# The third dense piece of the odd pairs in a forgetting attention layer moves from behind the fourth tile's transposes to before them

## What is computed

```python
def odd_mixer(h, w_in, b_f, qnorm_g, knorm_g, w_out):
    proj = (h @ w_in).astype(jnp.float32)
    q, k, v, g, fl = jnp.split(proj, [FOX_WIDTH, 2 * FOX_WIDTH, 3 * FOX_WIDTH, 4 * FOX_WIDTH], axis=-1)
    q = rms_norm(hd(q), qnorm_g).transpose(0, 2, 1, 3)
    k = rms_norm(hd(k), knorm_g).transpose(0, 2, 1, 3)
    logf = jax.nn.log_sigmoid(fl + b_f.astype(jnp.float32))
    cumf = jnp.cumsum(logf, axis=1).transpose(0, 2, 1)
    for blk in range(s_ // FOX_BLOCK):
        ...
        logits = (jnp.einsum('bhqd,bhkd->bhqk', q[:, :, q0:q1], k[:, :, :q1]) * scale
                  + cumf[:, :, q0:q1, None] - cumf[:, :, None, :q1])
        mask = jnp.arange(q0, q1)[:, None] >= jnp.arange(q1)[None, :]
        probs = jax.nn.softmax(jnp.where(mask, logits, -jnp.inf), axis=-1)
        outs.append(jnp.einsum('bhqk,bhkd->bhqd', probs, v[:, :, :q1]))
    o = jnp.concatenate(outs, axis=2).transpose(0, 2, 1, 3).reshape(b_, s_, FOX_WIDTH)
    o = o * jax.nn.silu(g)
    return o.astype(h.dtype) @ w_out
```

## Time and profile before

| what | value |
|---|---|
| median of 3 runs | 1705.82 us (1705.78 to 1706.29) |
| the profiled execution's own time | 1707.55 us |
| its span, first to last instruction | 1705.8 us |
| mean granted TensorE clock | 0.998 |
| TensorE matmuls busy | 1687.0 us, 99% |
| TensorE weight loads busy | 1396.9 us, 82% |
| VectorE, ScalarE, GpSimd busy | 1040.8, 759.3, 807.7 us |

### The profile page before, as it was taken

How to read it: one execution, slowest core, us unless ns; L and a number is a source line. 1 busy time by engine, 2 the same in 40 slices (tenths; PEclk the granted TensorE clock), 3 DMA queues, 4 the chain that set the end, 5 groups by cost and what they waited for, 6 DMA issues and landing times.

```text
span 1705.8 us, 25667 instructions
## 1 busy us (share of the span) xinstructions
PE 1687.0 (99%) x9753; PEld 1396.9 (82%) x9753; DVE 1040.8 (61%) x1717; ACT 759.3 (45%) x1332; POOL 807.7 (47%) x617
## 2 busy tenths in 40 slices
PE   9999999999999999999999999999999999999999
PEld 7777788888888888888888888887877888887887
DVE  5887567555564872664475555678377844237752
ACT  4443644222222354664532222234544457666650
POOL 6635236555555473232465555553532335453342
PEclk9999999999999999999999999999999999999999
DMA  9735237444445243222274444442322133334522
GB/s 369 253 138 201 84 124 271 173 170 164 163 158 194 99 136 112 87 83 92 98 272 173 172 172 172 172 165 82 99 75 69 51 100 100 106 89 129 160 89 74
DMA packets 114833, 242.72 MB, mean 142 GB/s; under 512 B 6144, under 2 KB 27776, under 8 KB 114736
## 3 DMA queue, kind: packets, MB, share of 16 engines
q1 hardware_dynamic: 112560, 237.20, 40.3%
q10 hardware_dynamic: 2176, 4.19, 0.8%
HBM read 239.21 MB, written 2.16 MB: 141 GB/s over the span
## 4 chain that ended last, share of the span: by engine, by line
PE 87%; DVE 6%; DMA 2%; ACT 2%; issue 1%; POOL 1%; SPq 0%; DVEq 0%; POOLq 0%; ACTq 0%
PE bank L242 40%; PE bank L656 20%; PE bank L1674 5%; PE bank L1640 3%; PE bank L453 3%; PE bank L432 2%; PE bank L1642 2%; DMA ct<-cumd 1%; PE bank L1758 1%; PE bank L416 1%; PE bank L1722 1%; PE bank L1234 1%; PE bank L1746 1%; PE bank L2253 1%; DVE fP L1850 1%
## 5 line engine op out<-in xcount | busy, mean ns | idle before, releaser
L2755 POOL TENSOR_TENSOR wsp<-raw,wsp 128x512 fp32r<-128x512 f32 x516 | 761.7, 1508 | 803.4 <-ACT wsp L197 803.4
L242 PE MATMUL bank<-xT,wsp 128*128 128x512 f32 x2016 | 464.9, 390 | 0.0
L242 PEld LDWEIGHTS bank<-xT,wsp 128*128 128x128 f32 x2016 | 377.7, 188 | 80.0 <-issue 0.9
L197 ACT ACTIVATE wsp<-raw 128x1024 fp32r<-128x1024 f32 x131 | 138.8, 1060 | 464.0 <-PE bank L656 240.3
L656 PE MATMUL bank<-wsp,hT 128*128 128x512 f32 x1344 | 308.2, 389 | 0.0
L242 PE MATMUL bank<-wsp,xT 128*128 128x512 f32 x1248 | 299.9, 396 | 1.3 <-DVE tok L2519 0.9
L656 PEld LDWEIGHTS bank<-wsp,hT 128*128 128x128 f32 x1344 | 252.3, 188 | 52.4
L242 PEld LDWEIGHTS bank<-wsp,xT 128*128 128x128 f32 x1248 | 231.8, 189 | 54.8 <-issue 4.8
L874 DVE CUSTOM_DVE_ANT_0 ada_ring<-ada_ring,crow,cols 128x1024 f32<-128x1024 f32 x96 | 148.4, 1580 | 4.5 <-DMA ada_ring<-in_ada_rows 4.5
L200 ACT ACTIVATE wsp<-raw 128x1024 fp32r<-128x1024 f32 x131 | 137.2, 1047 | 0.0
L795 DVE TENSOR_TENSOR x<-bank,x 128x512 f32<-128x512 f32 x80 | 55.2, 690 | 110.5 <-PE bank L656 110.5
(11 more groups left out here) (351 smaller groups left out, 2161.1 us busy)
## 6 DMA issues: line engine op xcount, KB each, us to landing
raw<-in_ff_w SPq DMA_DIRECT2D x64, 1024.0 KB, 5.2
ada_ring<-in_ada_rows SPq DMA_DIRECT2D x96, 512.0 KB, 6.3
tok<-in_ada_rows SPq DMA_DIRECT2D x32, 512.0 KB, 5.5
raw<-in_odd_w_in SPq DMA_DIRECT2D x16, 1024.0 KB, 5.4
raw<-in_gla_w_in SPq DMA_DIRECT2D x12, 1024.0 KB, 7.2
raw<-in_att_w_in SPq DMA_DIRECT2D x12, 1024.0 KB, 5.2
raw<-in_even_w_in SPq DMA_DIRECT2D x12, 1024.0 KB, 5.2
ring_s<-in_ada_rows SPq DMA_DIRECT2D x16, 512.0 KB, 11.0
```

The source lines that it names most:

```text
L197: act.activation(home[:, 0, 0:HK // 2], raw[:, slot, 0:HK // 2], ACT.Copy).then_inc(hi_part, 1)
L242: mm = pe.matmul(out_ap, l, r, start=(start and a == b), stop=(stop and a == 1))
L2755: ins = pool.tensor_tensor(w[:, 1, k], raw[:, slot, k], w[:, 0, k].bitcast(F32), ALU.subtract)
```

## The change

In the forgetting layer the third dense piece of a pair always stands between the third and the fourth tile's transposes. Before, it stood there only where the piece was a quarter of a tile (`quarters`, pairs 0, 2, 4 and 6), and behind all transposes otherwise.

```diff
                 quarters = u + 2 in work and work[u + 2][6] - work[u + 2][5] == KT // ST
                 for w in range(u, u + ST):
-                    if w == u + 3 and quarters:
+                    if w == u + 3 and (quarters or not ahead):
                         dense(u + 2)
                     turned(w)
-                if not quarters:
+                if not quarters and ahead:
                     dense(u + 2)
                 dense(u + 3)
```

## The result

| | before | after |
|---|---|---|
| median of 20 runs | 1705.93 us | 1708.64 us |
| lowest to highest | 1704.02 to 1709.86 | 1706.59 to 1710.48 |
| profiled execution, its own time | 1707.55 us | 1709.76 us |
| its span | 1705.8 us | 1708.0 us |

The ratio of the two kernels is 1.0014, with a 95% interval of 1.0008 to 1.0021: the change costs 2.4 us, between 1.4 and 3.6. The forecast was 1.8 us and "within 0.2%"; 1.8 us lies inside that interval, so the times alone don't tell it from 2.4. The medians themselves lie 2.7 us apart. The runs of one kernel spread over 4 to 6 us, far more than the 0.5 us of the three runs that I had seen.

A forecast was written before the change was run, and what follows sets the result against it. TensorE, busy for 99% of the span, was taken as the bound. Pairs 1, 3, 5 and 7 add 0.72 + 0.37 + 0 + 0.72 = 1.81 us to the median of 1705.82, giving 1707.6 us; range 1706.1 to 1709.0.

The forecast's parts named there:

- the delay of pair 5 is not absorbed: Rival, 15%: pair 5's delay reaches the end, +0.75 us and up to 0.8 of transfer either way, 1708.4 us.
- an unchanged 1.1 us wait in pair 7 with the end later by 2.5: Sign of a wrong forecast: pair 7's wait for VectorE stays 1.1 us and the end comes 2.5 us later.
- The wait for VectorE is not hidden: Third tile's transposes wait for all four tiles (shared PSUM banks), so the moved piece covers no wait; gain 0.
- The cut: One more transpose block and dense block in each changed pair, costing 0.14 + 0.23 = 0.37 us.
- A free cut: Rival, 10%: matmul spacing depends on columns alone, only uncovered transposes in pairs 1 and 7 cost; 0.7 us, 1706.5.
- weight loads and row groups: TensorE: the skill page lets a weight load run beside a matmul only where row groups differ; no size given.
- The wait for the bank: Moved piece waits for bank 0: about 0.34 us in pair 1, none in pair 3; pair 7 delayed about 0.72 us.
- Pair 5 costs nothing: Pair 5's delay of about 0.75 us shortens pair 7's 1.1 us VectorE wait to about 0.4; net cost 0.
- The clock: Granted clock was 1.00 in pair 2, which is cut the same way, so nothing was added; no chance of its own.
- The late copy: Rival, 4%: ScalarE's late copy of tiles 3 and 4 stalls scores in pairs 2, 4, 6; 4.5 us, 1710.3.

The follow-up runs named there:

- filled: Against the kernel with only pair 7 moved: eight extra 128 x 128 TensorE matmuls between pair 7's first and second tiles' transposes; ratio 1.0008 (0.9999 to 1.0017).
- the bias loads first: Pair 7's bias loads issued before the output weights' transfer: kernel before 0.9997, no piece between 1.0001, changed kernel 1.0007.

## Why the prediction was right, and where not

The direction, the class and most of the places were right; the size was 0.6 us short, though the interval holds the forecast too. The measured median of 1708.64 us lies inside the range of 1706.1 to 1709.0, but 1.0 us above the forecast and nearer to the 1708.4 of the rival *the delay of pair 5 is not absorbed*. The prediction also named its own sign of being wrong, an unchanged 1.1 us wait in pair 7 with the end later by 2.5, and the first profile shows very nearly that: 1.15 us, and an own time that is 2.2 us longer. So two terms that were put at 0, pair 5 and the clock, failed, and the range held because it left room for the first; for the second it left none, and that is luck.

- *The wait for VectorE is not hidden*: right. It stands before the third tile's transposes in all five profiles with pair 7 moved and not filled, at 0.83 to 1.15 us, and before 4 transposes instead of 16.
- *The cut*: right. 0.31 us in pair 3 (forecast 0.37), and 0.36 to 0.38 when taken away in pairs 2, 4 and 6. A free cut is refuted here. The prediction took that rule from the Trainium skill, TensorE: Matmul & The Clock Gate (Back-to-back issue gap); the page gives the spacing by columns alone for an isolated matmul and says that in a stream the weight load counts too, so what failed is the use made of it. What the prediction says of weight loads and row groups stands in that page's section The mechanism; no term of the sum rests on it.
- *The wait for the bank*: right. A wait of 0.26 us in pairs 1 and 7, and the piece starts 0.60 us after the third tile does. From the third tile on, pair 1 costs 0.67 us (6.98 against 6.31) and pair 7 0.70 (9.34 against 8.64), with 0.72 forecast for each (the terms given for pair 7 add up to 0.70). The whole of pair 1 took 15.39 to 15.93 us moved and 14.60 to 15.00 not moved; the 0.2 us beyond the cut is a longer wait for VectorE ahead of the moved piece, where the kernels are the same. In both, the 12 transposes that ran under the gate before now stand behind it.
- *Pair 5 costs nothing*: partly wrong. Moving it costs 0.73 us locally (18.10 to 18.33 against 17.41 to 17.53), as forecast. But what pair 7 gives back varied: from its scores to the third tile it took 8.61 to 9.74 us in the five profiles with pair 5 moved, 9.27 in the mean, and 9.37 to 9.82, 9.61 in the mean, in the seven others. That is 0.3 us returned of 0.73, so pair 5 costs about 0.4 us instead of 0. The two ranges overlap and the profiles are few, so 0.4 is an estimate and anything from nearly nothing to the whole 0.73 us fits. The step that failed took the wait of 1.1 us in one execution for steady slack. It isn't: bias loads that land later, or VectorE's low part beside GpSimd, take it up. Nor was all of the wait slack: 8.61 us from pair 7's scores to its third tile is what is left when the mask holds nothing (pair 5 alone), and that leaves a wait of 0.37 us, so the slack before was 9.44 - 8.61 = 0.83 us, just enough for pair 5's 0.73. The mask is part of the trouble as well: it took 1.93 to 1.99 us in the nine profiles in which VectorE's L2145 ran beside it, and 1.48 or 1.49 in the four in which it was done or nearly done by then. The chain of waits in the changed kernel shows the later landing:

```profile
1598.68 0.36 SPq L2158
...
1600.11 8.44 DMA ct<-cumd
...
1615.04 6.81 DMA ct<-cumd
...
1623.47 5.43 POOL wsp L2755 x4
1628.92 0.37 SPq L166
1629.34 1.35 SPq L2158
...
1631.83 7.92 DMA ct<-cumd
```

  Against the earlier trace rows, the first transfer is 0.44 us longer, the second 0.35 shorter and the last 0.45 longer. The conversion is 0.42 longer, but the mask before it took 1.48 us instead of 2.02, so that goes even. One issue took 1.35 us where it took 0.51, all four together 2.96 instead of 2.34. From pair 5's issue to pair 7's mask it is 41.5 us instead of 40.4. With pair 7's mask that late, nothing is absorbed. Whether the moved piece itself makes the chain longer stays open: it is 40.31 to 41.52 us in the four profiles with pair 5 moved and the old order of the loads, and 40.09 to 40.68 in the six others.
- *The clock*: wrong. I took the clock of pair 2, cut in the same way, and added nothing. But pair 2 waits for only 0.28 us. That can't be all, though. Pair 0 of the kernel before has nearly the two waits of the moved pair 7 (its second is the 0.26 us of the earlier trace rows), and keeps its clock; here its third tile, and the 3.68 us from its piece to the next scores:

```profile
1546.10 0.34 PE L1746 MATMUL bank<-ident,fP 64*128 64x64 f32 x4 [1.01 <-DVE fP L1859]
```

```profile
1546.70:1550.38 3.68, 3.68 (x26) 2.54 (x26) 2.00 (x4) 1.04 (x2) 0.17 (x1) 1.00 0.88 239
```

  The same stands in all eleven profiles with that piece between, 1.01 or 1.02 and 0.26 us, and the clock read 1.00 in each. What tells the two pairs apart, the 0.1 us of the first wait or the 12 dense matmuls before it instead of 24, was not tested. In pair 7 the granted clock fell in three of the five profiles with the piece moved and not filled, and in none of the seven where it stays behind the transposes, five of which had the same wait of 1.14 or 1.15 us before the third tile. The fall costs 1.6 us each time. Three of five against none of seven is suggestive and not proof; the two runs of pair 7 alone, at 2.0 and 2.6 us for a local 0.7, say the same by another way. That it can be chance is shown near 167 us, long before the changed stage, where all the kernels are the same: ten profiles have a wait of 1.65 to 1.67 us there, the clock fell in four of them, and all four are kernels with pair 7 not moved. So the second wait as the cause is argued, not shown.
- *The late copy*: right that it has 3 us to spare (in the changed kernel ScalarE's copy of pair 1 ends at 1562.02 us, and the scores that need it start at 1564.93). No scores waited for ScalarE in any run.

The sum with what was measured: 0.7 + 0.3 + 0.4 + 0.7 = 2.1 us with the clock up, and 1.6 x 3/5 = 1.0 more for its falls, 3.1 in the mean of so few profiles; the runs say 2.4 (1.4 to 3.6). How often the clock falls in a run without profile stays open, and with it how the 2.4 us divide. What is shown is the part that stands in every profile: the cuts and the waits for the bank in pairs 1, 3 and 7, 1.7 us.

Neither form with the opposite change beat the kernel before by what can be measured: 0.9995 (0.9986 to 1.0004) for no piece between, and 1.0001 (0.9992 to 1.0010) with the bias loads first. In the profile of the first the stage is 0.6 us shorter.

## What to carry to other kernels

Count the blocks before moving a piece between others: on TensorE, when it is full, each further block cost 0.14 us (transposes) to 0.23 us (dense matmuls) here, and it pays only if a wait really stands at the new place, which a shared bank can put one step earlier. A wait seen once is not slack; look at what holds the next link when the first comes sooner. And look at the granted clock behind a new short wait beside a long one: where it falls, as it did in three profiles here, the fall costs more than the wait, though these runs don't prove that the wait brings it about.

## What I had not expected of the hardware

- The granted clock fell to 0.50 after 1.15 us idle, 0.34 us of transposes and 0.26 us idle, in three of four profiles with just these waits (1.13 to 1.15 us for the first); with the first wait alone it stayed at 1.00 in all five, and with 1.01 or 1.02 and 0.26 us in pair 0 in all eleven. Behind a single wait of 1.65 to 1.67 us near 167 us it fell in four profiles of ten. The same code with the same waits can go either way.
- VectorE's L2145, both of whose inputs lie in SBUF, took 1.86 us when it started at 1640.70 and GpSimd's L2755 at 1640.72; in the kernel with pair 5 moved it started at 1639.83, 0.13 us ahead of GpSimd's, and took 0.70. By the Trainium skill, SBUF — State Buffer (SBUF: two separate sides), such an instruction and one of GpSimd that reads SBUF exclude each other for a whole instruction, and whichever starts first has the ports. The trace agrees in its size: the lengthening of 1.2 us is about one instruction of L2755 (5.03 us for four), and in all three kernels with the bias first VectorE's ends 1.83 or 1.84 us after GpSimd's first has started. With pair 5 moved it is GpSimd that gets longer, 5.47 us for its four. As for the order, 0.02 us are too little to say which started first in the first case.
- The bias transfers, 6.81 to 8.57 us each in the chains of waits, made the way from pair 5's issue to pair 7's mask 40.09 to 41.52 us long from profile to profile, in the kernels with the old order of the loads; that is as much as most terms of the sum.
